# Doubled sample tokens and four 32-row state updates in a two-layer hybrid decoder step

## The reference

```
C:  S_new = exp(BL)[..., None] * S + einsum('bshk,bshv->bhkv', kc * exp(BL - Bc), vc)
B:  S_new = chunk_dec * S          + einsum('hs,bshk,bshv->bhkv', to_end, kc, vc)
A:  C_new = dec * C                + einsum('bhs,bshk,bshv->bhkv', w_s, kc, vc)
```

## Time and profile before

| | |
|---|---|
| three runs | 1529.33, 1530.03, 1530.54 us, median 1530.03 |
| profiled execution | 1529.52 us, of which span 1527.7 us |
| PE busy | 98% of the span |
| DVE / ACT / POOL busy | 63% / 44% / 62% |
| DMA | mean 146 GB/s |
| chain that ended last | PE 90%, DVE 5%, ACT 2%, DMA 2%, issue 1% |
| mean granted TensorE clock | 0.997 |

### The profile page before, as it was taken

One profiled execution on the slowest core, in us unless ns is written; L12 is line 12 of the kernel. 1 busy time (PEld: TensorE's weight loads), 2 busy tenths in 40 slices (PEclk: granted clock), 3 DMA queues, 4 the chain that ended last, 5 costly groups with the idle time before them and its releaser, 6 DMA issues.

```text
span 1527.7 us, 26521 instructions
## 1 busy us (share of the span) xinstructions
PE 1501.1 (98%) x10325; PEld 1449.0 (95%) x10325; DVE 959.8 (63%) x1942; ACT 679.8 (44%) x1240; POOL 951.7 (62%) x741
## 2 busy tenths in 40 slices
PE   9999999999999999999999999999999999999997
PEld 8999899999999999999999999999999999999997
DVE  4664356777876777744345644567778677777334
ACT  5734444444444544433357344444444445444333
POOL 7666445555556666777767665554555566777774
PEclk9999999999999999999999999999999999999999
DMA  8434453434545444444434335443454354444542
GB/s 290 125 125 122 145 183 117 163 130 139 176 152 161 140 138 146 144 153 151 152 111 139 115 107 200 152 140 112 146 184 149 113 167 125 152 151 140 155 150 88
DMA packets 66549, 223.38 MB, mean 146 GB/s; under 512 B 8056, under 2 KB 12664, under 8 KB 66424
## 3 DMA queue, kind: packets, MB, share of 16 engines
q1 hardware_dynamic: 66424, 221.67, 45.6%
HBM read 206.07 MB, written 15.58 MB: 145 GB/s over the span
## 4 chain that ended last, share of the span: by engine, by line
PE 90%; DVE 5%; ACT 2%; DMA 2%; issue 1%; SPq 0%; POOL 0%; DVEq 0%; ACTq 0%
PE gps L1392 26%; PE gps L1394 26%; PE gps L1393 26%; PE xp L1639 2%; PE xp L1583 1%; PE xp L1641 1%; DMA raw<-in_w 1%; PE xp L1544 1%; PE xp L1631 1%; PE xp L1554 1%; PE xp L1533 1%; DVE s L1179 1%; PE gps L1533 1%; DVE zc L1069 0%; PE xp L1562 0%
## 5 line engine op out<-in xcount | busy, mean ns | idle before, releaser
L645 POOL TENSOR_TENSOR wlo<-raw,whi 128x512 fp32r<-128x512 f32 x724 | 944.2, 1327 | 557.4 <-ACT whi L666 358.8
L1392 PE MATMUL gps<-xh,whi 128*128 128x320 f32 (+1 forms) x2000 | 638.3, 319 | 6.6 <-DVE zc L929 3.5
L1394 PE MATMUL gps<-xh,wlo 128*128 128x320 f32 (+1 forms) x2000 | 621.3, 311 | 0.0
L1393 PE MATMUL gps<-xl,whi 128*128 128x320 f32 (+1 forms) x2000 | 620.8, 310 | 0.0
L666 ACT ACTIVATE whi<-raw 128x1024 fp32r<-128x1024 f32 x272 | 287.2, 1056 | 353.0 <-PE gps L1394 285.0
L1392 PEld LDWEIGHTS gps<-xh,whi 128*128 128x128 f32 x2000 | 377.3, 189 | 15.1 <-DVE zc L929 4.2
L1393 PEld LDWEIGHTS gps<-xl,whi 128*128 128x128 f32 x2000 | 378.6, 189 | 3.2
L1394 PEld LDWEIGHTS gps<-xh,wlo 128*128 128x128 f32 x2000 | 378.3, 189 | 0.0
L1392 PE MATMUL gps<-ah,whi 128*128 128x320 f32 x640 | 199.2, 311 | 0.5 <-DVE al L979 0.3
L1393 PE MATMUL gps<-al,whi 128*128 128x320 f32 x640 | 197.8, 309 | 0.0
L1394 PE MATMUL gps<-ah,wlo 128*128 128x320 f32 x640 | 197.7, 309 | 0.0
(11 more groups left out here) (314 smaller groups left out, 1830.7 us busy)
## 6 DMA issues: line engine op xcount, KB each, us to landing
raw<-in_w SPq DMA_DIRECT2D x360, 512.0 KB, 3.5
s<-in_st SPq DMA_DIRECT2D x24, 512.0 KB, 4.3
out_ss<-s SPq DMA_DIRECT2D x24, 512.0 KB, 2.7
con<-in_cst SPq DMA_DIRECT2D x4, 462.0 KB, 5.5
out_sp<-pst SPq DMA_DIRECT2D x24, 64.0 KB, 2.6
mix<-in_x SPq DMA_DIRECT2D x4, 320.0 KB, 5.2
out_y<-mix SPq DMA_DIRECT2D x8, 160.0 KB, 1.9
raw<-in_w SPq DMA_DIRECT2D x4, 256.0 KB, 5.0
```

The source lines that it names most:

```text
L645: nc.gpsimd.tensor_tensor(wlo[:, c % RING, half, :], raw[:, c % RING, half, :], whi[:, c % RING, half, :].bitcast(F32), ALU.subtract).then ...
L1392: M(out, hi, xhi, start=start, stop=False)
L1393: M(out, hi, xlo, start=False, stop=False)
L1394: return M(out, lo, xhi, start=False, stop=stop)
```

## The change

The third tile of a transpose now holds the sample tokens twice, in rows 0 to 63 and again in 64 to 127, for v and for k. In `turn` a third full transpose takes columns 192 to 319 (its lower half is the sample), and a fourth, of 64 columns, writes the sample over the upper half. ACT copies each result with one instruction of 128x384, and POOL's clearing and its semaphore are gone. In the `fin` phase `vm` has 128 rows and two copies in place of 64 rows and four; there is one matmul for each of the four groups of 32 rows, into `xp1`, `xp2`, `xp3` and the second half of `xp0`. Group g holds the sequences from 4*(g mod 2) + 2*(g div 2). DVE updates the states group by group, and in B one instruction does both sequences of a group. The masks are built for both halves, in two instructions each.

```diff
-NQ = 32 // DS
+GROUPS = 4
+NQ = NB // GROUPS
...
+        def state_group(g):
+
+            first = 4 * (g % 2) + NQ * (g // 2)
+            return first, (xp[1], xp[2], xp[3], xp[0])[g][:, 256 * (g // 3):256 * (g // 3) + NQ * P]
...
-            zero_pads()
...
-                    pool.wait_ge(slot_done, c - c % NSLOT)
-                    zero_pads()
...
-                    act.wait_ge(pad_zero, 2 * (layer + 1))
-                    nc.scalar.activation(v[:, b, 0:2, :], bank[:, 0:2 * P].rearrange("p (a c) -> p a c", a=2), ACT.Copy)
-                    nc.scalar.activation(v[0:NS, b, 2, :], bank[0:NS, 2 * P:3 * P], ACT.Copy).then_inc(free, 1)
+                    nc.scalar.activation(v[:, b, :, :], bank[:, 0:3 * P].rearrange("p (a c) -> p a c", a=3),
+                                         ACT.Copy).then_inc(free, 1)
...
-                    nc.scalar.activation(kt[:, 0:2, :], xp[0][:, 0:2 * P].rearrange("p (a c) -> p a c", a=2), ACT.Copy)
-                    nc.scalar.activation(kt[0:NS, 2, :], xp[0][0:NS, 2 * P:3 * P], ACT.Copy)
+                    nc.scalar.activation(kt[:, :, :], xp[0][:, 0:3 * P].rearrange("p (a c) -> p a c", a=3), ACT.Copy)
...
-                return V.tensor_tensor(vm[:, :, :], v_of(n, h, 2).unsqueeze(1).to_broadcast([NS, NQ, P]),
+                return V.tensor_tensor(vm[:, :, :], v_of(n, h, 2).unsqueeze(1).to_broadcast([P, NQ, P]),
...
-                    for b in range(NB):
-                        new = xp[1 + b // 4][:, (b % 4) * P:(b % 4 + 1) * P]
-                        keep = (1.0 - 2.0 ** (-5 - h)) ** DS if n == "B" else dec[:, h, b:b + 1]
+                    for g in range(GROUPS):
+                        first, new = state_group(g)
+                        each = NQ if n == "B" else 1
+                        for b in range(0, NQ, each):
+                            old = s0[:, j % 2, first + b:first + b + each, :]
...
-                            V.tensor_tensor(same[:, :], c_("seqmask", NS)[:, 0:NQ], c_("seqmask", NS)[:, NQ:NB], ALU.add)
-                            V.tensor_tensor(fade[:, :, :], each[:, :, 0:NQ], each[:, :, NQ:NB], ALU.add)
+                            for r in range(2):
+                                rows, lo = slice(NS * r, NS * (r + 1)), NQ * r
+                                V.tensor_tensor(same[rows, :], c_("seqmask", NS)[:, lo:lo + NQ],
+                                                c_("seqmask", NS)[:, 4 + lo:4 + lo + NQ], ALU.add)
+                                V.tensor_tensor(fade[rows, :, :], each[:, :, lo:lo + NQ], each[:, :, 4 + lo:4 + lo + NQ], ALU.add)
...
-                for i, (lo, n) in enumerate(TILES):
-                    last = nc.tensor.transpose(out_bank[0:n, i * P:(i + 1) * P], src[:, lo:lo + n], ident)
-                return last
+                for i in range(2):
+                    nc.tensor.transpose(out_bank[:, i * P:(i + 1) * P], src[:, i * P:(i + 1) * P], ident)
+
+                nc.tensor.transpose(out_bank[:, 2 * P:3 * P], src[:, T - P:T], ident)
+                return nc.tensor.transpose(out_bank[0:NS, 2 * P:3 * P], src[:, SEQ:T], ident)
...
-                    for j in range(0, NQ, 2):
-                        for i in range(2):
-
-                            rows = slice(32 * i, 32 * (i + 1))
-                            M(xp[1 + i][:, j * P:(j + 2) * P], kt[rows, 2, :], vm[rows, j:j + 2, :], start=True,
-                              stop=True, tile_position=(32 * i, 0), skip_group_check=True)
+                    for g in range(GROUPS):
+
+                        rows = slice(32 * g, 32 * (g + 1))
+                        M(state_group(g)[1], kt[rows, 2, :], vm[rows, :, :], start=True, stop=True,
+                          tile_position=(32 * g, 0), skip_group_check=True)
```

More of the change, by code:

```diff
@@ L401, in trunk @@
         ee = sb("ee", [P, SP4])
[L402 to L405, removed]
+        vm = sb("vm", [P, NQ, P])
+        own = sb("own", [P, NQ])
+        same = sb("same", [P, NQ])
+        fade = sb("fade", [P, H, NQ])
         kt = sb("kt", [P, 3, P])
@@ L462, in trunk @@
         x_hi, x_lo = sem("x_hi"), sem("x_lo")
-        pad_zero = sem("pad_zero")
         dve_chain, act_chain = sem("dve_chain"), sem("act_chain")
@@ L482, in v_of @@
         def v_of(n, h, tile):
-            rows = TILES[tile][1]
-            return (va if n == "A" else vc)[0:rows, h, tile, :]
+            return (va if n == "A" else vc)[:, h, tile, :]
+        def state_group(g):
+            first = 4 * (g % 2) + NQ * (g // 2)
+            return first, (xp[1], xp[2], xp[3], xp[0])[g][:, 256 * (g // 3):256 * (g // 3) + NQ * P]
         def state_of(n, h):
@@ L616, in _ @@
             nc.gpsimd.memset(iff[:, :, :], 0.0).then_inc(setup_pool, 1)
-            def zero_pads():
-                nc.gpsimd.memset(vc[:, :, 2, :], 0.0).then_inc(pad_zero, 1)
-                nc.gpsimd.memset(va[:, :, 2, :], 0.0).then_inc(pad_zero, 1)
-            zero_pads()
             def shift(q):
@@ L1047, in spread_values @@
                     ends, mask = (ee[:, 255:256], ee[:, 383:384]), own[:, :]
-                    half = 384 + NQ * DS
-                    link(V.tensor_tensor(own[:, :], ee[0:NS, 384 + DS - 1:half:DS], ee[0:NS, half + DS - 1:SP4:DS],
-                                         ALU.add))
+                    ends_of = ee[0:NS, 384 + DS - 1:SP4:DS]
+                    for r in range(2):
+                        last = V.tensor_tensor(own[NS * r:NS * (r + 1), :], ends_of[:, NQ * r:NQ * (r + 1)],
+                                               ends_of[:, 4 + NQ * r:4 + NQ * (r + 1)], ALU.add)
+                    link(last)
                 elif n == "B":
@@ L1060, in spread_values @@
                     V.tensor_copy(vw[:, :, P], ee[:, 255:384:128])
-                return V.tensor_tensor(vm[:, :, :], v_of(n, h, 2).unsqueeze(1).to_broadcast([NS, NQ, P]),
-                                       mask.unsqueeze(2).to_broadcast([NS, NQ, P]), ALU.mult)
+                return V.tensor_tensor(vm[:, :, :], v_of(n, h, 2).unsqueeze(1).to_broadcast([P, NQ, P]),
+                                       mask.unsqueeze(2).to_broadcast([P, NQ, P]), ALU.mult)
             def phase(stage, n, h, k, layer, done):
@@ L1175, in phase @@
                         V.tensor_tensor(nou[:, h, 1:1 + NB], nou[:, h, 1:1 + NB], xp[0][:, P + 1:P + 1 + NB], ALU.add)
-                    for b in range(NB):
-                        new = xp[1 + b // 4][:, (b % 4) * P:(b % 4 + 1) * P]
-                        keep = (1.0 - 2.0 ** (-5 - h)) ** DS if n == "B" else dec[:, h, b:b + 1]
-                        last = V.scalar_tensor_tensor(out=s0[:, j % 2, b, :], in0=s0[:, j % 2, b, :], scalar=keep,
-                                                      in1=new, op0=ALU.mult, op1=ALU.add)
+                    for g in range(GROUPS):
[3 more added lines that the diff above has]
+                            old = s0[:, j % 2, first + b:first + b + each, :]
+                            keep = (1.0 - 2.0 ** (-5 - h)) ** DS if n == "B" else dec[:, h, first + b:first + b + 1]
+                            last = V.scalar_tensor_tensor(out=old, in0=old, scalar=keep,
+                                                          in1=new[:, b * P:(b + each) * P].rearrange("p (b c) -> p b c", c=P),
+                                                          op0=ALU.mult, op1=ALU.add)
                     done(last)
```

## The result

The changed kernel takes 1521.55 us (median of 4 runs, 1521.06 to 1521.89) against 1530.23 us for the kernel before (4 runs, 1529.33 to 1530.54). The ratio is 0.9943, with a 95% interval from 0.9931 to 0.9955. That is 8.7 us less where 5.2 was forecast, and outside the range (1522.3 to 1530.2) on the side of the larger gain. The direction was right, the size was not. Medians are compared only with runs of the kernel before made beside them, since its own median lies between 1529.25 and 1531.53 us from one set of runs to the next.

What follows compares the result with a forecast made beforehand. PE, busy for 98% of the span, was taken to bound the kernel. 1529.52 - 10.0 + 4.6 + 0.2 = 1524.3 us, with 0.5 for the profiled execution lying under the median 1524.8 us; range 1522.3 to 1530.2.

Steps and rivals of the forecast that it cites:

- The `fin` gain: PE's state matmuls start four at a time, two steps instead of four: 0.42 us per phase, 10.0 us less.
- the price of the transposes: One more transpose in each of 48 `turn` calls at 0.11 us of PE time: 5.3 us more before hiding.
- The cover at the waits for `seen`: At six PE waits behind transposes, the added transpose disappears in the wait: 0.7 us covered, leaving 4.6 us more.
- Rival 1: In `fin`, four groups come two by two and the 10.0 us are gone: 1534.8 us; chance 0.07.
- Rival 2: In `fin`, four start together but each step lengthens to 0.32 us, losing 5.0 us: 1529.8; chance 0.11.
- Rival 3: In `turn`, the fourth transpose waits for the third's writes, costing 0.19 us: 3.4 us more, 1528.2; chance 0.07.
- the stretched step: In `fin`, a four-fold step of 0.28 us by the skill's factor: gain 7.2 us, 1527.6; no separate chance given.
- What is off the path: Changes to ACT copies, POOL clears and DVE updates were taken to leave PE's time unchanged: 0 us.
- The setup: DVE's mask building in layer 0 lies on the path; two small added instructions cost 0.2 us, between 0.1 and 0.4.
- The drop to the lower level: Lower clock at 52 to 60 us, losing 1.7 us, forecast to stay; could go or recur, 1.7 us either way.

Runs made afterwards that it cites:

- transposes_only: Kernel before with only the doubled third tile: four transposes per turn, single ACT copies, no POOL clears; 1533.07 us against 1529.25.
- two_row_groups: Changed kernel with the fin matmuls on two row groups alternately, still writing four banks; 1531.58 us against 1529.25 for the kernel before.
- groups_only: Changed kernel with the old transposes, ACT copies and POOL clears, so some states lack their sum; 1518.54 us against 1529.25 for the kernel before.
- normalizer_behind: Kernel before with DVE's small normalizer multiply moved behind the state update for heads 0 to 2 of A; 1530.30 us against 1531.53.
- after_again: The changed kernel measured once more, unaltered, as a reference; 1521.84 us against 1531.53 for the kernel before.
- pool_quarters: Kernel before with POOL's wlo instructions of 256 columns in place of 512; 1526.71 us against 1531.11.
- dve_heavier: Changed kernel with B's update in eight instructions again and the vm multiply issued twice; 1520.82 us against 1529.25 for the kernel before.
- act_two_copies: Changed kernel with each of ACT's 48 copies in two instructions again; 1521.48 us against 1531.11 for the kernel before.

## Why the prediction was wrong

**What held.** The `fin` gain (10.0 forecast, 10.0 measured) and the price of the transposes (5.3 forecast, 5.2 measured) came out to a tenth, both in the changed kernel and alone. The cover at the waits for `seen` was about 0.8 us where 0.7 was forecast (below). Rivals 1, 2 and 3 did not happen, and neither did the stretched step that I had worked out beside it from the factor of 3.07 in the Trainium skill, "TensorE: Matmul & The Clock Gate", Part 3: the second step starts 0.32 us after the first (157.26 to 157.58), as before, and L1644 0.33 after that (0.31 before).

**The step that failed** is the paragraph "What is off the path", with its sum of 0 us. I took everything behind the `fin` as a chain of fixed length that moves with it, and counted only two kinds of waits near the change. The four waits of PE's weight loads for the update of A and the one of `a_cum` were in the trace, and I left them out. These five waits went, 1.6 us. The chain has no fixed length, because DVE's instructions with two SBUF inputs are held while POOL works, so their time depends on when they come. Behind the mark the sum was to be 10.0 - 44 x 0.11 + 0.7 = 5.9 us, and 8.3 were measured in the first profile. The difference of 2.4 lies in three waits, read from the distances of PE's starts: four times `a_score`, 1.1 us; the wait of `a_cum` in layer 1, 0.5; and the waits for `seen` with the weight load behind them, 1.6 in place of 0.7. Against these 2.5 us stand 0.4 lost at two branch projections that wait for DVE's `tt`, and a few tenths either way in the rest. The `a_cum` wait has the same cause. In the kernel before:

```profile
968.59 2.53 POOL L645 TENSOR_TENSOR wlo<-raw,whi 128x512 fp32r<-128x512 f32 x2 [1.48 <-DVE whi L912]
...
970.49 0.67 DVE L1101 SCALAR_TENSOR_TENSOR af<-iff,af 128x12 f32<-128x12 f32 x1 [0.77 <-ACT af L749]
...
971.30 0.36 PE L1592 MATMUL xp<-af,con 128*128 128x4 f32 x2 [0.43 <-DVE af L1101]
```

Twelve columns end at 971.16, POOL at 971.12. After the change this instruction takes 0.17 us in both layers and the wait is not in the list. It is absent in transposes_only and two_row_groups as well, and present, 0.4 to 0.5 us, in groups_only and normalizer_behind, where the instruction takes 0.63 and 0.72 us and again ends 0.03 us after POOL's. So here it is the shift by the transposes that removed it.

The 1.6 us at the waits for `seen` have three parts, read place by place. First, outside four heads (at 167, 183, 1060 and 1089 us in the kernel before) 1.06 us are given back, and 1.05 to 1.07 in after_again, transposes_only and two_row_groups too; in groups_only and normalizer_behind, which have no added transposes, it is 0.3 and 0.2. So about 0.8 us is the cover of the transposes, and 0.2 to 0.3 belongs to the one profile of the kernel before. Last, 0.4 us is at 167 and 183 us, and moves with DMA landings: on the same chain as the earlier trace rows the weight DMA took 4.44 us before and 4.77 after, on the next one 4.73 before, and the wait is nearly gone after. In after_again all these waits gave 1.2 us.

I call the `a_score` part shown (by two_row_groups, normalizer_behind and pool_quarters), and the `a_cum` part and the cover shown by which kernels have them. Of the rest at `seen`, some 0.8 us, only the size is known.

**The setup** was forecast at 0.2 us. DVE's timeline of the changed kernel, which answers to the earlier trace rows:

```profile
42.07 0.19 DVE L1366 TENSOR_TENSOR same<-con 64x2 f32<-64x2 f32 x1
...
42.36 1.16 DVE L1366 TENSOR_TENSOR same<-con 64x2 f32<-64x2 f32 x1
43.45 0.15 DVE L1368 TENSOR_TENSOR fade<-con 64x8 f32<-64x8 f32 x1
```

The second `same` was held for 1.16 us, again by POOL, whose instruction ends at 43.51, this one at 43.52. PE then waits 1.8 us for `mix`, where it waited 0.4. It cost little at the end, because the wait of the earlier trace rows at 55 us shrank from 2.5 to 1.4 in two_row_groups, dve_heavier and act_two_copies, which have the same setup; counted from a dense matmul at 38 us, their starts behind it are 0.3 us later than in the kernel before, which is near the forecast. In the changed kernel's first profile that wait is gone and the starts are 0.5 us later, with the lower clock described next.

**The clock.** In the profile of the changed kernel the granted clock was 0.79 between 6 and 14 us and 0.86 between 44 and 56, but 1.00 behind. The stretches (busy by engine, clock, DMA share, GB/s), to set beside the earlier trace rows:

```profile
6.00:14.00 8.00, 6.21 (x32) 5.98 (x32) 4.69 (x11) 5.25 (x11) 4.43 (x4) 0.79 0.79 304
44.00:56.00 12.00, 10.24 (x59) 9.98 (x58) 11.22 (x16) 8.07 (x15) 6.40 (x5) 0.86 0.36 102
56.00:62.00 6.00, 5.88 (x40) 5.62 (x39) 3.34 (x5) 3.54 (x8) 4.69 (x4) 1.00 0.40 150
```

The drop to the lower level, 1.2 GHz, behind the long wait, which the forecast kept, is gone: it had cost 1.5 us in the kernel before (48 matmuls of the slots from 55.73 on take 8.7 us there and 7.2 in each of the other thirteen profiles). Two others came. The first cost about as much (the first 48 matmuls of the slots take 10.5 us, and 9.0 before). The second stands where PE otherwise waits 1.4 us, and cost 0.2. So in this pair the losses nearly cancel, and that the start came out near the forecast is in part luck. The mark is reached between 77.5 and 79.3 us in the eleven profiles with POOL's instructions of 512 columns, and between 75.7 and 76.4 in the three with smaller ones; PE's work up to it differs by 0.4 us at most. The profiled pair differs by 7.6 us (1529.52 and 1521.89) and the medians by 8.7, and the missing 1.1 us is within this scatter of the start. With one profile of the kernel before I can't attribute it.

**The range** had its low end at 1522.3 because I gave every secondary effect a loss or nothing. The waits that PE already had, 16 us in all, were a place where a gain of 2 to 3 us could come from, and the range should have reached that far down.

## What to carry to other kernels

A matmul over 32 rows leaves three quarters of the array idle. Four groups of them on different rows, each into a bank of its own, started in steps as long as those of two groups here, and doubling the operand for it cost half of what it gained. Where a small DVE instruction with two SBUF inputs stands on a chain and takes several times its shortest duration, look at what POOL runs beside it before calling the chain's length fixed: an edit that shifts one against the other by a few tenths can change it. An edit on the bounding engine should be counted by the distances of its starts; its second effects are in the waits, and they can go either way.

## What the hardware showed that I had not expected

- DVE waits for POOL's running instruction to end: 0.91 us for 8 columns against 0.155 at least, and 44 us of DVE's 959.8 us busy time vanished when POOL's instructions were halved from 512 to 256 columns (mean 1327 to 767 ns; POOL's own busy time rose from 951.7 to 1073.1 us).
- Four row groups of 32 rows with 128 output partitions each ran in steps as long as two did, 0.42 us less a phase, and a transpose that overwrites the one before it starts after the same 0.11 us. The step next to a change between 128 and 32 rows is 0.32 us, the one without 0.215.
- Smaller POOL instructions gave 4.4 us on the kernel before and none on the changed one, whose profile shows the start 1.5 us shorter and the rest longer.
